# Prompt attention: score rows longer than 512 columns handed over and masked by halves, each PSUM bank freed by its own half

## The reference

```python
causal = kpos[None, :] <= (n * Q_BLOCK + jnp.arange(Q_BLOCK))[:, None]
p1 = softmax(where(causal, einsum('bqhd,bkhd->bhqk', qb[..., :64], k1), NEG))
p2 = softmax(where(causal, einsum('bqhd,bkhd->bhqk', qb[..., 64:], k2), NEG))
o  = einsum('bhqk,bkhd->bqhd', p1 - lam * p2, vf)
```

## Time and profile before

| | us |
|---|---|
| median of 3 runs | 2663.31 |
| lowest, highest run | 2659.84, 2664.61 |
| the profiled execution | 2665.06 |
| its span in the trace | 2662.9 |
| prompt attention, from the first score matmul to the last exponential | 536.5 to about 810 |
| PE busy over the span | 2508.2 (94%) |
| DVE, ACT, POOL busy | 1064.8, 674.7, 193.5 |

### The profile page before, as it was taken

How to read it: one execution, slowest core, us unless ns; L and a number is a source line. 1 busy time by engine, 2 the same in 40 slices (tenths; PEclk the granted TensorE clock), 3 DMA queues, 4 the chain that set the end, 5 groups by cost and what they waited for, 6 DMA issues and landing times.

```text
span 2662.9 us, 40057 instructions
## 1 busy us (share of the span) xinstructions
PE 2508.2 (94%) x16305; PEld 2307.1 (87%) x16305; DVE 1064.8 (40%) x2217; ACT 674.7 (25%) x1180; POOL 193.5 (7%) x233
## 2 busy tenths in 40 slices
PE   7999979888889989999999999989899999999997
PEld 6778756645559989999999999989899999999996
DVE  4312055555675533333233333447233333333324
ACT  5221123355574321111111111154111111111112
POOL 0020000044332000000000000030000000000000
PEclk9999989999998999999999999998999999999998
DMA  4331279964553011110111111111111111111101
GB/s 158 107 105 46 113 260 387 345 184 130 174 190 98 1 64 48 48 47 30 37 48 48 32 49 48 33 45 32 48 33 48 48 48 48 48 48 48 47 8 67
DMA packets 120144, 229.56 MB, mean 86 GB/s; under 512 B 6771, under 2 KB 82852, under 8 KB 117419
## 3 DMA queue, kind: packets, MB, share of 16 engines
q1 hardware_dynamic: 114451, 180.28, 20.0%
q0 software_dynamic: 5536, 46.96, 5.1%
HBM read 209.32 MB, written 51.41 MB: 98 GB/s over the span
## 4 chain that ended last, share of the span: by engine, by line
PE 85%; issue 7%; DVE 5%; ACT 3%; POOL 0%; DMA 0%; SPq 0%; DVEq 0%; ACTq 0%
PE ps L1770 70%; PE ps L768 2%; PE ps L1804 2%; PE ps L803 2%; PE ps L784 2%; PE ps L1857 2%; PE ps L1871 1%; ACT dkT L1154 1%; DVE dse L1488 1%; PE ps L2072 1%; PE ps L1881 1%; DVE ws L613 1%; DVE pT L567 0%; ACT dse L1170 0%; POOL sm L1050 0%
## 5 line engine op out<-in xcount | busy, mean ns | idle before, releaser
L1770 PE MATMUL ps<-xn,ws 128*128 128x384 f32 (+1 forms) x6744 | 1123.2, 327 | 21.8 <-DVE ws L613 15.9
L1770 PEld LDWEIGHTS ps<-xn,ws 128*128 128x128 f32 x6744 | 1116.1, 189 | 24.9 <-issue 24.1
L1770 PE MATMUL ps<-hh,ws 128*128 128x384 f32 (+1 forms) x3168 | 539.0, 330 | 8.7 <-issue 8.7
L1770 PEld LDWEIGHTS ps<-hh,ws 128*128 128x128 f32 x3168 | 532.9, 190 | 9.2 <-issue 9.2
L1605 DVE TENSOR_TENSOR act_h<-act_s,ps 128x384 f32<-128x384 f32 x132 | 70.3, 533 | 875.2 <-ACT act_s L1233 875.2
L1233 ACT ACTIVATE act_s<-ps 128x384 f32<-128x384 f32 x132 | 62.6, 474 | 1233.9 <-PE ps L1770 1124.0
L1592 DVE TENSOR_TENSOR x<-ps,x 128x384 f32<-128x384 f32 (+1 forms) x552 | 285.1, 533 | 210.5 <-PE ps L1770 208.8
L1770 PE MATMUL ps<-wp,xn 128*128 128x512 f32 (+1 forms) x1080 | 245.4, 389 | 0.0
L1770 PEld LDWEIGHTS ps<-wp,xn 128*128 128x128 f32 (+1 forms) x1080 | 196.3, 182 | 48.9
L613 DVE TENSOR_TENSOR ws<-wraw,ws 128x2048 fp32r<-128x2048 f32 x69 | 157.4, 2283 | 8.8 <-ACT ws L608 8.8
L608 ACT ACTIVATE ws<-wraw 128x2048 fp32r<-128x2048 f32 x69 | 129.5, 1904 | 46.8 <-PE ps L1770 44.8
(11 more groups left out here) (206 smaller groups left out, 1784.3 us busy)
## 6 DMA issues: line engine op xcount, KB each, us to landing
wraw<-w_gate SPq DMA_DIRECT2D x22, 1024.0 KB, 5.3
wraw<-w_up SPq DMA_DIRECT2D x22, 1024.0 KB, 5.4
wraw<-w_down SPq DMA_DIRECT2D x22, 1024.0 KB, 4.9
kraw<-cache_win_k_a SPq DMA_DIRECT2D x8, 2048.0 KB, 11.7
vraw<-cache_win_v_a SPq DMA_DIRECT2D x8, 2048.0 KB, 9.8
kraw<-cache_k_b SPq DMA_DIRECT2D x64, 256.0 KB, 4.0
vraw<-cache_v_b SPq DMA_DIRECT2D x64, 256.0 KB, 6.8
o_wk_s<-cache_win_k_a POOLq DMA_DIRECT2D x8, 2032.0 KB, 8.8
```

Source lines behind the costliest of these rows:

```text
L1770: r = mm(out, w(a), m(b_), start=(i == 0 and q_ == 0), stop=(i == n - 1 and q_ == 2))
```

## The change

A unit of i >= 4 has two halves c = 0, 1: columns 0 to 511 and the rest. (1) PE raises `scores_done` after each half (both s). (2) DVE waits for a half, masks it for s = 0 and s = 1, then the other half: four mask instructions instead of two, each with its own memset, and each with its own row result. (3) After the four, DVE waits for them itself and joins the two results of a row by a minimum, one small instruction for each s; those minima now raise `scores_masked`, for which ACT's exponentials wait. (4) PE waits before each half of its scores, and only for the mask that last read the same bank (`bank_reader`), by the new semaphore `halves_masked` where that was a half of a long unit. Units i < 4 keep one instruction for each s.

```diff
+        def bank_reader(u, c):
+            pair, mix, i, n = unit_at(u)
+            before = 8 * pair + (-1, -1, 0, 1, 2 + c, 4, 5, 6)[i]
+            if before < 0:
+                return None
+            if before % 8 < 4:
+                return scores_masked, 2 * before + 2
+            return halves_masked, 4 * (4 * (before // 8) + before % 8 - 4) + 2 * (i % 2 if i < 4 else c) + 2
...
-                dve.wait_ge(scores_done, u + 1)
                 if u >= 4:
                     dve.wait_ge(probs_turned, last_group(u - 4) + 1)
-                for s in range(2):
-                    bank = score_bank(i, s)
-                    dve.memset(small[:, 12 + 2 * (u % 2) + s:13 + 2 * (u % 2) + s], 0.0)
-                    dve.tensor_tensor_reduce(sm[:, u % 4, s, 0:n], ps[:, bank:bank + 1 + i // 4].rearrange("p a n -> p (a n)")[:, 0:n],
-                                             pmask[:, mix, S - n:S], 1.0, 3.0e38, ALU.add, ALU.min, pstat[:, u % 4, s, 0:1]).then_inc(scores_masked, 1)
+                for c in range(halves(u)):
+                    dve.wait_ge(scores_done, halves_up_to(u) + c + 1)
+                    c0, cn = 512 * c, min(512, n - 512 * c)
+                    for s in range(2):
+                        spare = 12 + 4 * (u % 2) + 2 * c + s
+                        dve.memset(small[:, spare:spare + 1], 0.0)
+                        dve.tensor_tensor_reduce(sm[:, u % 4, s, c0:c0 + cn], ps[:, score_bank(i, s) + c, 0:cn],
+                                                 pmask[:, mix, S - n + c0:S - n + c0 + cn], 1.0, 3.0e38, ALU.add, ALU.min,
+                                                 pstat[:, u % 4, s, c:c + 1]).then_inc(halves_masked if i >= 4 else scores_masked, 1)
+                if i >= 4:
+                    dve.wait_ge(halves_masked, 4 * (4 * pair + i - 4) + 4)
+                    for s in range(2):
+                        st_ = pstat[:, u % 4, s]
+                        tt(st_[:, 0:1], st_[:, 0:1], st_[:, 1:2], ALU.min).then_inc(scores_masked, 1)
...
-                masked_before = 8 * pair + (0, 0, 1, 2, 4, 5, 6, 7)[i]
-                if masked_before:
-                    pe.wait_ge(scores_masked, 2 * masked_before)
                 for c0, s in pieces:
+                    if s == 0 and bank_reader(u, c0 // 512):
+                        pe.wait_ge(*bank_reader(u, c0 // 512))
...
-                if pieces[-1] == score_pieces(u)[-1]:
-                    q_.then_inc(scores_done, 1)
+                    if s:
+                        q_.then_inc(scores_done, 1)
```

More of the change, by code:

```diff
@@ L309, in build_step @@
         scores_masked = sem("scores_masked")
+        halves_masked = sem("halves_masked")
         exps_ready = sem("exps_ready")
@@ L510, in last_group, with halves, halves_up_to @@
             return group_number[(u, s, k0)]
+        def halves(u):
+            return 1 + unit_at(u)[2] // 4
+        def halves_up_to(u):
+            return sum(halves(v) for v in range(u))
+        def bank_reader(u, c):
[6 more added lines that the diff above has]
+            return halves_masked, 4 * (4 * (before // 8) + before % 8 - 4) + 2 * (i % 2 if i < 4 else c) + 2
         def score_bank(i, s):
@@ L713, in prompt_act @@
                     act.wait_ge(dec_stored, 2 * DB)
-                    act.wait_ge(scores_done, 56)
+                    act.wait_ge(scores_done, halves_up_to(56))
                     act.activation(ssq[:], osam[:, 1].rearrange("p j n -> p (j n)"), ACT.Square).then_inc(sample_squares_ready, 1)
```

## The result

The changed kernel takes 2679.76 us (median of 5 runs, 2674.96 to 2681.94) against 2660.39 for the kernel before in the same comparison: a ratio of 1.0068, interval 1.0053 to 1.0083. The prediction was 2663.7, no change. The profiled execution of the changed kernel took 2678.3 us, 13.2 more than that of before; the medians lie 19.4 apart, as the profiled execution of before (2665.06) lies above the five runs beside it (2658.0 to 2664.61).

A forecast was written before the change was run, and what follows sets the result against it. No engine full, waits decide: PE stands 35.7 us before scores for DVE's masks. Terms -0.9 + 3 x 0.4 + 0.6 - 2 x 0.26 = +0.4 us on 2665.06, less 1.75 for the median: 2663.7, range 2655 to 2671.

The forecast's parts named there:

- The cuts: Long units' masks on DVE: each row cut in two costs 0.09 us more, 64 cuts 5.8 us of DVE time.
- order of halves: Units of i = 4 to 7: first exponential waits for both rows, 1.1 to 1.5 us later, 5.2 us a pair.
- the cycle: Second mixer, S(5) to S(5) of the next pair: 29.89 us against 30.15, 0.26 us a pair gained.
- pair 4: Pair with both head start and L581: mask(5) comes 0.3 us later, T(6) 0.6 us later.
- the path through a pair of the first mixer: First mixer, pairs 1 to 3: mask(7) 0.2 us earlier, exp(7) ends 1.3 later, +0.4 us a pair reaches S(4).
- the slack of 0.57: First mixer, ACT's copy following exp(7): it starts 0.57 us after ACT is free, so T(5)'s last group is 0.7 later.
- the 0.3 that DVE's waits were to take up: First mixer: of the 0.7 us delay of T(5)'s last group, about 0.3 is taken up where DVE waits.
- the clock, "2 us either way": Granted clock: waits at other places may shed or add dips near half speed, 2 us either way.
- The join in the first mixer: After the last half-mask an exponential starts 0.30 us later instead of 0.11, bounds 0.11 to 0.43, priced from the sample attention.
- PE no longer waits for whole units: First mixer after mask(5): the loop is quicker than before, 4.38 us to mask(6), about 5.4 to mask(7).
- The slower rival: exp(7) blocks T(5)'s copies on ACT if mask(7) starts no earlier: 6 to 10 us, 2669 to 2673, chance 0.18.
- The faster rival: Attention stage: bubbles close as late exponentials find slack; all 35.7 us gives 2627.6, half 2645; chance 0.22.

The follow-up runs named there:

- With the clock held: Changed kernel with spare score matmuls in PE's T(2) and T(5) waits, 2664.92 us, compared with the kernel before with two spare matmuls a turn, 2655.18 us.
- changed kernel with spare work: Changed kernel with spare score matmuls, computing nothing new, in PE's waits inside T(2) and T(5) of the first mixer: 2664.92 us, 1.0008 to the kernel before.
- row-by-row order: Changed kernel masking both halves of s = 0, their minimum, then s = 1, each exponential waiting for its own row: 2656.74 us, 0.9981 to the kernel before.
- the join (10 us back): Changed kernel with the two minima written with one tensor and one number a row (tensor_scalar) instead of tensor_tensor: 2669.6 us, 1.0024 to the kernel before.
- ACT's order (16): Changed kernel with q's copy and the output copies ahead of the exponentials on ACT: 2663.99 us, 1.0002 to the kernel before.

## Why the prediction was wrong, by its own steps

*Right.* The cuts: half-masks start 0.62 us apart for 512 columns and 0.22 for 128, so a cut costs the 0.09 of the forecast. In the second mixer the exponential starts 1.98 us after mask(4)'s start, as computed (join and order of halves as predicted); the cycle was 0.16 off; PE's wait went from before S(5) to before T(6); pair 4 lost 0.8 (0.6). Timelines of the changed kernel, DVE, then ACT:

```profile
743.97 0.69 DVE L550 CUSTOM_DVE_ANT_0 sm<-ps,pmask 128x512 f32<-128x512 f32 x1
...
745.76 0.23 DVE L557 TENSOR_TENSOR pstat<-pstat 128x1 f32<-128x1 f32 x2
```

```profile
745.95 0.83 ACT L697 ACTIVATE sm<-sm,pstat 128x640 f32<-128x640 f32 x1 [1.33 <-DVE pstat L557]
```

Two steps failed, and together they make the 13.8 us.

*The first failed step: the path through a pair of the first mixer, "+0.4 us a pair".* With the clock held it is 2.2, so 6.6 in three pairs instead of 1.2. The forecast had mask(7) 0.2 us earlier after S(4) and exp(7) ending 1.3 later. In the changed kernel with spare work mask(7) starts 639.47 - 620.87 = 18.60 us after S(4), in the kernel before 601.25 - 583.28 = 17.97: 0.6 later. The second exponential ends 24.36 us after S(4) instead of 21.54: 2.8 later. Less the slack of 0.57 that ACT has there, 2.2 reach S(4); the 0.3 that DVE's waits were to take up were not taken up. Two terms make the 1.5 between 1.3 and 2.8. One is mask(7), 0.8 later than forecast: mask(5) came 0.2 later, mask(6) 4.75 us after it instead of 4.38, for the join of i = 5, and mask(7) 5.63 after that instead of about 5.4. The other is the join of i = 7, below. The kernel before (ACT), then the changed kernel with spare work (DVE, ACT):

```profile
603.67 1.15 ACT L672 ACTIVATE sm<-sm,pstat 128x1024 f32<-128x1024 f32 x1
```

```profile
639.47 0.69 DVE L550 CUSTOM_DVE_ANT_0 sm<-ps,pmask 128x512 f32<-128x512 f32 x1
```

```profile
644.09 1.14 ACT L697 ACTIVATE sm<-sm,pstat 128x1024 f32<-128x1024 f32 x1
```

*The second failed step: the clock, "2 us either way".* It measured 5.8 in the stage. One dip was in view, but it was priced as noise and not as something that the moved waits could multiply. The forecast moved PE's waits from before the scores to inside the transposes and summed their lengths; what they would cost there at the lower level, no step asked.

*The join in the first mixer: 0.30, between 0.11 and 0.43.* From the mask's start the exponentials of i = 4 to 7 come 2.19, 2.61, 3.04 and 3.46 us later (pair 2: for i = 7, 648.98 - 645.52), instead of 1.98, 2.24, 2.50, 2.78: the join costs 0.51, 0.67, 0.84, 0.98 instead of 0.30. For i = 7, DVE, then ACT:

```profile
645.52 0.69 DVE L550 CUSTOM_DVE_ANT_0 sm<-ps,pmask 128x512 f32<-128x512 f32 x1
```

```profile
648.98 1.15 ACT L697 ACTIVATE sm<-sm,pstat 128x1024 f32<-128x1024 f32 x1 [3.17 <-DVE pstat L557]
```

The row that priced it comes from a place where POOL is idle. The 1.8 us a pair that this adds were outside the bounds, and taking them away gave 10 us.

*The wait left out.* "PE no longer waits for whole units" in the first mixer was true of the scores. But T(2)'s second group needs the bank that q's copy empties, that copy stands behind exp(4) on ACT, and S2(5), q's next transposes and V(1) stand behind T(2) on PE: 1.57 us. With the output's low part (2.70 us idle on DVE before it, 2.01 in the earlier trace rows) mask(5) came 1.2 later than before (1.0 predicted), and mask(7) 19.13 us after S(4) in pair 2, where 17.8 was predicted; with the clock held it is 18.60. In pair 0, which was to gain 0.9 us and lost 0.6 with the clock held, T(2) waits for q's copy too, 1.44 us.

*The slower rival* named the right place, exp(7) ahead of T(5)'s copies, and its condition (mask(7) late) held in the first mixer; at 0.9 to 1.4 us a pair it was nearer to the 2.2 of the first mixer than the forecast; but its 6 to 10 us counted the second mixer too, where pairs 5 to 7 lost nothing, and had no clock in them either. *The faster rival* has its chance in the row-by-row order: the bubbles do close, by 2 us a pair of the second mixer, when the first exponential need not wait for both rows. The Trainium skill says that breaking up instructions may let work end sooner where these engines cause bubbles on others (Perfetto Trace Analysis, section "Optimizing Scalar/DVE Operations"). In the row-by-row order the time agrees (2656.74 us), in the change as made it does not (2679.76).

The chain of causes is shown by runs that cut it at four points: the join (10 us back), the order of the halves (23), ACT's order (16), idle PE (15). They overlap, so they don't add up. Open stays what decides whether a wait is followed by a dip, and why a part of what comes back lies outside the stage.

## What to carry to other kernels

When a change moves waits of the bounding engine, ask where they collect, and price the granted clock with the waits. The lost clock that a table of stretches gives is an upper bound; filling PE's waits with spare matmuls, in the kernel before as well as after, tells the clock's share from the schedule's. Cut a row only if its consumer can still start on the first finished row, and follow what stands behind that consumer in its engine's order. Price a small added instruction from a row with the same neighbours on the other engines, not only the same shape.

## What the hardware showed unexpectedly

- The same wait of 1.78 us before S(0) has no dip behind it at 603.78 and 642.20 in the kernel before, and one at 680.61 (0.52 in the earlier trace rows): one wait's length doesn't decide. The two others of that kernel:

```profile
642.20 0.49 PE L768 MATMUL ps<-qk 64*128 64x128 f32 x4 [1.78 <-DVE pstat L531]
...
680.61 0.49 PE L768 MATMUL ps<-qk 64*128 64x128 f32 x4 [1.78 <-DVE pstat L531]
```

- A dip of the clock worth at most 1.6 us lengthened its pair by 0.5 (41.15 against 40.64 us).
- A two-operand minimum of one number a row took 0.84 us beside POOL's multiply, 0.15 without.
- Spare matmuls, which compute nothing new, made the kernel before 0.26% faster.
